# Two networks in one program on one core: both ends of the expert layer rewritten, and gate and up weights loaded as 512 rows by 1024 columns

## The chip, the cores and the metric

The kernel runs on one core of a Trainium2 chip, in one launch. The metric is the device time of that launch in microseconds. Times "before" are the median of three runs; a profile is one execution of its own.

## What is computed

A first block (two layers of dilated attention and gated scans) feeds a second one. Each of the second block's two layers has a mixer (gated delta rule and sparse attention), then a feed-forward part: dense in layer 0, eight experts in layer 1. There are 256 tokens of 1024 features, all in float32. What the change touches is the end of layer 1:

```python
x = x + g_m * y
h = rms_norm(x, norm_ffn[l]) * (1.0 + sc_f) + sh_f
...
def moe_ffn(h, w_router, w1, w3, w2):
    logits = (h @ w_router).astype(jnp.float32)
    top_val, top_idx = lax.top_k(logits, TOP_K)            # TOP_K = 2 of N_EXPERTS = 8
    top_w = jax.nn.softmax(top_val, -1)
    combine = jnp.sum(jax.nn.one_hot(top_idx, N_EXPERTS, dtype=jnp.float32) * top_w[..., None], -2)
    out = jnp.zeros_like(h)
    for e in range(N_EXPERTS):
        out = out + combine[..., e:e + 1].astype(h.dtype) * swiglu(h, w1[e], w3[e], w2[e])
    return out
...
x = x + g_f * f
```

`swiglu(h, w1, w3, w2)` is `(silu(h @ w1) * (h @ w3)) @ w2`, with a hidden width of 3584. The weights of one expert are 44 MB.

## The kernel before

**Weights.** All weights pass through RING, seven slots of 2 MB in SBUF. SP issues one DMA per slot, in the order in which TensorE uses them, and waits on `item_used` until the block that held the slot seven blocks ago is used up (L2847). A gate or up block is 1024 rows by 512 columns of a matrix whose rows are 3584 floats long, so each piece that lies together in memory is 2 KB. A down block is 512 whole rows of 1024 floats, 4 KB each.

**Routing.** At the end of the mixer DVE gates the product with GATE_ROW and adds it to X, one tile of 128 tokens at a time (L2282, L2284). Then `pe_entry`, `act_entry` and `dve_entry` make h: ACT squares X and sums, ACT and DVE form one over the root of the mean, DVE makes a diagonal matrix of it (DIAG), TensorE multiplies X by the diagonal and transposes by it (L1320), and ACT and DVE apply scale and shift while they take the result out of PSUM into HT. TensorE multiplies HT by `router_w` (L2292). DVE finds the two best experts of each token (L2312 to L2330), and TensorE counts tokens and finds each one's place in its expert's list (L2297 to L2301). DVE sorts the experts by their number of tokens (`rank_key`, `rank_sorted`, `rank_i`). With `ranked` SP reads the first and the last expert of that order into registers (L2834) and issues the first expert blocks. DVE forms the places by rank, the selection matrices SEL (L2411) and all weights, and clears ACC (L2392); all engines meet in `phase(..., "ffn")`; TensorE gathers the tokens by a matmul with SEL (L2435), and ACT takes them out into HTG (L2442).

**A turn.** One turn handles a pair of experts, one with many tokens and one with few: 64 tokens each side by side ("wide", L2555 and L2584), and up to 64 more (turn 0) or 32 more (later turns) of the first one ("extra", L2568 and L2594). Here there are four turns: turn 0 is written out, the others are one loop. A turn goes over seven slices of 512 hidden columns. For each: gate (bank 0 of PSB), up (bank 1), with the extra part of both in bank 2; ACT applies silu (L2643), DVE multiplies (L2682), TensorE transposes (L2575), ACT copies (L2651), and down of the slice before adds into PSA. Six blocks a slice, 42 a turn, 168 in all. Bank 3 is for odd jobs ("misc"): the last turn's rows are scattered back into ACC through it (L2450, added by DVE at L2456), SELW is transposed and the next turn's tokens are gathered. In the last turn a gather is made for a turn that doesn't come.

**The end.** After the loop all engines meet again, four scatters run, DVE adds them to ACC, multiplies ACC by GATE_ROW (L2701), adds it to X (L2703), and SP stores X, 1 MB, in one DMA (L2870).

## Time and profile before

| what | us |
|---|---|
| median of three runs | 2612.45 (2610.32 to 2614.62) |
| the profiled execution, its own time | 2612.26 |
| its span, first to last instruction | 2610.5 |
| TensorE busy | 2460.1 (94%) |
| VectorE (DVE) busy | 614.0 (24%) |
| ScalarE (ACT) busy | 455.7 (17%) |

The span is what the views below divide; the execution's own time is 1.8 us longer. "Busy" counts instructions of an engine, not its sequencer's waits. In the rows DMA share is the mean busy share of the 16 DMA engines, and PEclk the granted share of TensorE's full clock. A float32 matmul stands as two rows of the trace.

### The profile page before, as it was taken

Reading aid. Unit: us, or ns where it says so; the run is one execution under the profiler, and the core shown is the slowest. Engines: PE = TensorE matmul, PEld = TensorE weight load, DVE = VectorE, ACT = ScalarE, POOL = GpSimd, SP = SyncE. Lnnn points to the kernel's source line nnn. Section 1 sums busy time; section 2 is a strip of 40 time slices with the busy share of each in tenths; the row PEclk is TensorE's granted clock in tenths of the full one; section 3 lists DMA queues with packets and bytes.
Section 4 is the critical chain, followed back from the end, with each engine's and each line's share of the span. In section 5 each row is a group of like instructions: output and inputs, shape, how many; then the busy total and the mean of one; then the engine's idle time right before and its main releaser. Section 6 shows DMA issues by size and latency. Waiting matters only on the chain.

```text
span 2610.5 us, 36347 instructions
## 1 busy us (share of the span) xinstructions
PE 2460.1 (94%) x15945; PEld 1437.8 (55%) x15945; DVE 614.0 (24%) x1457; ACT 455.7 (17%) x949; POOL 48.2 (2%) x67
## 2 busy tenths in 40 slices
PE   7999999999999999999999999799999889989987
PEld 5754776756685547777677655444443334333333
DVE  1241556713444320000144332300000001001001
ACT  1321123322213310000122142200010000001000
POOL 3300000000000000000000000000000000000000
PEclk9999899998999999999999999799999999999999
DMA  8633633327224137434532521399999999999995
GB/s 255 127 129 105 233 133 137 129 105 258 67 99 161 65 111 276 151 140 175 190 89 98 194 93 37 112 393 394 394 393 394 393 394 394 391 396 388 389 393 212
DMA packets 258237, 586.58 MB, mean 225 GB/s; under 512 B 14592, under 2 KB 16720, under 8 KB 258080
## 3 DMA queue, kind: packets, MB, share of 16 engines
q1 hardware_dynamic: 254304, 576.93, 60.2%
q0 software_dynamic: 3376, 5.94, 1.4%
q8 instruction: 130, 2.13, 0.3%
q10 hardware_dynamic: 400, 1.36, 0.2%
q14 instruction: 27, 0.22, 0.0%
HBM read 583.14 MB, written 1.06 MB: 224 GB/s over the span
## 4 chain that ended last, share of the span: by engine, by line
PE 84%; DMA 8%; SPq 3%; DVE 2%; ACT 1%; issue 1%; DVEq 1%; ACTq 0%
PE PSA L325 15%; PE PSB L2555 12%; PE PSA L340 10%; PE PSB L2489 7%; DMA RING<-in_w_moe 7%; PE PSA L2584 5%; PE PSA L2471 4%; PE PSB L2568 4%; PE PSA L699 3%; SPq L2847 3%; PE PSA L1278 2%; PE PSA L1901 2%; PE PSA L2594 2%; PE PSB L1470 1%; PE PSA L1852 1%
## 5 line engine op out<-in xcount | busy, mean ns | idle before, releaser
L2555 PE MATMUL PSB<-RING,Y 128*64 128x512 f32 x1792 | 399.9, 599 | 41.1 <-issue 20.8
L325 PE MATMUL PSA<-RING,HT 128*128 128x512 f32 (+1 forms) x896 | 392.5, 587 | 8.6 <-ACT Y L1441 5.0
L340 PE MATMUL PSA<-HT,RING 128*128 128x256 f32 x1216 | 277.8, 389 | 8.6 <-DMA RING<-in_w_in_ab 4.2
L2555 PEld LDWEIGHTS PSB<-RING,Y 128*64 128x64 f32 x1792 | 133.2, 138 | 270.4 <-issue 258.0
L325 PEld LDWEIGHTS PSA<-RING,HT 128*128 128x128 f32 x896 | 165.7, 191 | 183.2 <-issue 178.0
L340 PEld LDWEIGHTS PSA<-HT,RING 128*128 128x128 f32 x1216 | 235.0, 195 | 45.1 <-issue 11.7
L2584 PE MATMUL PSA<-RING,ROW 128*64 128x512 f32 x896 | 198.4, 595 | 5.6 <-issue 4.3
L2489 PE MATMUL PSB<-HT,RING 128*128 128x256 f32 x896 | 199.8, 381 | 2.0 <-DMA RING<-in_w_dense 2.0
L2489 PEld LDWEIGHTS PSB<-HT,RING 128*128 128x128 f32 x896 | 171.2, 191 | 37.2 <-issue 12.4
L2682 DVE TENSOR_TENSOR ROW<-ROW,PSB 128x512 f32<-128x512 f32 (+2 forms) x56 | 28.2, 504 | 589.7 <-PE PSB L2555 553.0
L2568 PE MATMUL PSB<-RING,Y 128*32 128x128 f32 (+1 forms) x3136 | 132.9, 289 | 0.0
L2568 PEld LDWEIGHTS PSB<-RING,Y 128*32 128x32 f32 (+1 forms) x3136 | 103.8, 114 | 52.3 <-issue 39.0
L2584 PEld LDWEIGHTS PSA<-RING,ROW 128*64 128x64 f32 x896 | 64.5, 137 | 120.2 <-issue 118.4
L2651 ACT ACTIVATE ROW<-PSB 128x512 f32<-128x512 f32 (+2 forms) x56 | 25.1, 450 | 503.0 <-PE PSB L2575 502.9
L2471 PE MATMUL PSA<-RING,PROJ 128*128 128x512 f32 x224 | 100.5, 592 | 0.0
L2508 DVE TENSOR_TENSOR PROJ<-PROJ,PSB 128x256 f32<-128x256 f32 x28 | 11.8, 421 | 277.2 <-PE PSB L2489 277.2
L2643 ACT ACTIVATE ROW<-PSB 128x512 f32<-128x512 f32 (+2 forms) x56 | 25.2, 450 | 283.9 <-PE PSB L2555 213.3
L1278 PE MATMUL PSA<-RING,small 128*32 128x512 f32 x384 | 57.1, 748 | 11.8 <-DVE X L709 5.0
L699 PE MATMUL PSA<-RING,HT 128*128 128x512 f32 x128 | 61.3, 634 | 5.1 <-ACT HT L383 5.1
L2471 PEld LDWEIGHTS PSA<-RING,PROJ 128*128 128x128 f32 x224 | 42.6, 190 | 42.1 <-issue 40.7
L2594 PE MATMUL PSA<-RING,ROW 128*32 128x512 f32 (+1 forms) x448 | 65.6, 597 | 0.0
L353 ACT ACTIVATE PROJ<-PSA 128x1024 f32<-128x1024 f32 x33 | 33.7, 1021 | 158.7 <-PE PSA L340 80.6
(444 smaller groups left out, 2256.8 us busy)
## 6 DMA issues: line engine op xcount, KB each, us to landing
RING<-in_w_moe SPq DMA_DIRECT2D x168, 2048.0 KB, 20.1
RING<-in_w_ada SPq DMA_DIRECT2D x24, 2048.0 KB, 8.1
RING<-in_w_dense SPq DMA_DIRECT2D x21, 2048.0 KB, 11.9
RING<-in_w_in SPq DMA_DIRECT2D x20, 2048.0 KB, 11.6
RING<-in_w_in_c SPq DMA_DIRECT2D x15, 2048.0 KB, 8.0
RING<-in_w_in_ab SPq DMA_DIRECT2D x10, 2048.0 KB, 15.6
RING<-in_w_out SPq DMA_DIRECT2D x4, 2048.0 KB, 7.8
RING<-in_w_out_ab SPq DMA_DIRECT2D x3, 2048.0 KB, 7.8
```

The source lines that it names most:

```text
L325: mm = pe.matmul(PSA[:, lane[k], 512 * t:512 * t + cols], HT[:, c, P * t:P * t + P], W[:, c, 0:cols], start=(c == 0), stop=(c == KC - 1))
L340: mm = pe.matmul(PSA[:, lane[k], S * j:S * j + S], W[:, c, P * j:P * j + P], HT[:, c, :], start=(c == 0), stop=(c == KC - 1))
L699: mm = pe.matmul(PSA[:, t, 512 * hf:512 * hf + 512], YT4[:, c, P * t:P * t + P], W[:, c, 512 * hf:512 * hf + 512], start=(first and c == 0 ...
L1278: mm = pe.matmul(PSA[r:r + 32, lane[k], 512 * a:512 * a + 512], cT[:, c:c + 1].broadcast_to([P, 32]), W[:, c, :], start=(c < 4), stop=(c > ...
L1901: mm = pe.matmul(PSA[:, t, 512 * hf:512 * hf + 512], YMT[:, 4 * n + c, P * t:P * t + P], W[:, c, 512 * hf:512 * hf + 512], start=(n == 0 a ...
L2471: mm = pe.matmul(PSA[:, t, 512 * hf:512 * hf + 512], HID[k % 2][:, P * t:P * t + P], W[:, q, 512 * hf:512 * hf + 512], start=(k == 0), sto ...
L2489: mm = pe.matmul(PSB[:, 2 * which + k % 2, 0:S], W[:, c, P * q:P * q + P], HT[:, c, :], start=(c == 0), stop=(c == KC - 1))
L2555: mm = pe.matmul((UP if up else GATE)[WIDE * which:WIDE * which + WIDE, :], HTG[:, c, WIDE * which:WIDE * which + WIDE], W[which][:, c, :] ...
L2568: mm = pe.matmul(BOTH[ec * j:ec * j + ec, c0:c0 + pw], HTG[:, c, P:P + ec], W[:, c, pw * j:pw * j + pw], start=(c == 0), stop=(c == KC - 1))
L2584: mm = pe.matmul(OUT[0][WIDE * which:WIDE * which + WIDE, 512 * hf:512 * hf + 512], HIDT[0][:, g % 2, q, WIDE * which:WIDE * which + WIDE] ...
L2594: mm = pe.matmul(OUT[1][ec * j:ec * j + ec, 512 * hf:512 * hf + 512], hid[:, b, j, :], W[0][:, q, 512 * hf:512 * hf + 512], start=(g == 0 ...
L2847: sp.dma_start(slot_view(j), src).then_inc(sem(f"slot_loaded{j % SLOTS}"), 16)
```

## The change

**Blocks and stages.** The seven slices are grouped in stages (0,1), (2,3), (4,5), (6). In a stage of two slices a gate or up block is 512 rows by 1024 columns, for both slices at once, so that its pieces are 4 KB; two such blocks per expert and matrix follow each other (`kh` = 0, 1). The last slice keeps the old shape. Gate and up of a stage use banks 0 and 1 of PSB, one for each slice, one after the other; bank 2 holds the extra part of both slices. Silu and product of the extra part are one instruction for both slices.

**Start.** The sums for scale and shift move ahead of the mixer's last product (`dve_moe_prepare`), where `router_w` is multiplied by the scale. Logits are taken from X itself, transposed but not normalized; DVE scales them per token by `rms_x` and adds `router_shift`. The second tile's gating and adding are done in halves. Counts are computed first and waited for alone, and `rank_key` follows. Weights of the tokens come behind the first selection. Clearing ACC and the meetings of all engines are gone; ACC is a copy of X instead.

**Rows.** DVE multiplies each turn's result by GATE_ROW as it takes it out of PSUM, where ACT and DVE copied it before.

**End.** The last turn is written out on its own. It gathers nothing. Its last two down blocks are loaded in two halves of 512 columns each, and gating, scattering, adding and storing go by halves and quarters.

```diff
+        STAGES = [range(g, min(g + 2, GROUPS)) for g in range(0, GROUPS, 2)]
         turn_items = []
-        for g in range(GROUPS):
-            turn_items += [(1, "gate", g), (0, "gate", g), (1, "up", g), (0, "up", g)]
-            turn_items += [(1, "down", g - 1), (0, "down", g - 1)] if g else []
-        turn_items += [(1, "down", GROUPS - 1), (0, "down", GROUPS - 1)]
+        for u, stage in enumerate(STAGES):
+            for kind in ("gate", "up"):
+                turn_items += [(which, kind, (u, kh)) for kh in range(len(stage)) for which in (1, 0)]
+            if u:
+                turn_items += [(which, "down", g) for g in STAGES[u - 1] for which in (1, 0)]
+        turn_items += [(which, "down", g) for g in STAGES[-1] for which in (1, 0)]
...
+        def dve_moe_prepare(dve):
...
+            dve.tensor_tensor(ROUTED, router_w[:, :, :], md[:, 0:8].unsqueeze(2).broadcast_to([P, KC, N_EXP]), ALU.mult)
+            dve.drain()
+            dve.tensor_reduce(router_shift, ROUTED.rearrange("p c e -> p e c"), AX.X, ALU.add)
+            dve.tensor_tensor(router_w[:, :, :], router_w[:, :, :], md[:, 8:16].unsqueeze(2).broadcast_to([P, KC, N_EXP]), ALU.mult)
...
         def pe_router(pe):
+            need(pe, "gate_spread")
             for t in range(NT):
+                for hf in range(2):
+                    if t == 0 and hf == 0 or t == 1:
+                        need(pe, "x_ready")
+                    for c in range(4):
+                        mm = pe.transpose(PSB[:, 2 * t + hf, P * c:P * c + P], X[:, t, 512 * hf + P * c:512 * hf + P * c + P], ident)
+                    mm.then_inc(sem("h_turned"), 1)
...
             need(pe, "chosen")
+            for t in range(NT):
+                mm = pe.matmul(COUNTS, CF[:, C_ONE:C_ONE + P], chosen[:, t, :], start=(t == 0), stop=(t == NT - 1))
+            mm.then_inc(sem("places"), 1)
...
+                dve.scalar_tensor_tensor(logits[:, t, :], PSA[:, 0, 512 * t:512 * t + N_EXP], rms_x[:, t:t + 1], router_shift,
+                                         ALU.mult, ALU.add)
...
-            def first_wide(kind, g):
...
+            def first(kind, u, kh):
...
+                if kind == "gate" and kh == 0:
+                    if u:
+                        pe.wait_ge(sem("moe_turned_taken0"), each(turn, STAGES[u - 1][-1]))
+                        pe.wait_ge(sem("moe_turned_taken1"), staged(turn, u - 1))
...
+                if kind == "up" and kh == 0:
+                    pe.wait_ge(sem("moe_silu0"), each(turn, STAGES[u][-1]))
+                per = KC // n
+                for i in range(n):
+                    for c in range(per * kh, per * kh + per):
+                        for which in range(2):
+                            mm = pe.matmul(WIDE_BANKS[i][WIDE * which:WIDE * which + WIDE, :],
+                                           HTG[:, c, WIDE * which:WIDE * which + WIDE], W[which][:, c - per * kh, 512 * i:512 * i + 512],
+                                           start=(c == 0), stop=(c == KC - 1))
                 mm.then_inc(sem("item_used"), 1)
...
+            for u, stage in enumerate(STAGES):
+                for kind in ("gate", "up"):
+                    for kh in range(len(stage)):
+                        first(kind, u, kh)
...
+                turned_wide(u)
+                for n, g in enumerate(STAGES[u - 1] if u else ()):
+                    if u == len(STAGES) - 1 and not end:
+                        misc(SCATTERS + 1 + n)
+                    down(g)
+                turned_extra(u)
+            if not end:
+                misc(SCATTERS + 3)
+                down(GROUPS - 1)
+                return
+            for hf in range(2):
+                pe.wait_ge(sem(f"last_columns{hf}"), 32)
+                down_wide(GROUPS - 1, (512 * hf,), False)
+                down_extra(GROUPS - 1, (512 * hf,)).then_inc(sem("last_rows"), 1)
+            pe.wait_ge(sem("misc_free"), pieces(turn, SCATTERS + 1))
+            for piece in LAST_PIECES:
+                pe.wait_ge(sem("moe_rows"), turn + (piece % 2 + 1))
+                scatter_piece(pe, piece, piece).then_inc(sem("last_rows"), 1)
...
-                        src = w[:, :, 512 * g:512 * g + 512].rearrange("a (k p) n -> p (a k) n", p=P)
+                        u, kh = g
+                        rows_, cols = D // len(STAGES[u]), 512 * len(STAGES[u])
+                        src = w[:, rows_ * kh:rows_ * kh + rows_, 1024 * u:1024 * u + cols].rearrange("a (k p) n -> p (a k) n", p=P)
...
+            for n, piece in enumerate(LAST_PIECES):
+                t, cols = piece // 2, slice(512 * (piece % 2), 512 * (piece % 2) + 512)
+                sp.wait_ge(sem("result"), n + 1)
+                sp.dma_start(out[0].rearrange("(t p) f -> p t f", p=P)[:, t, cols], ACC[:, t, cols]).then_inc(sem("out_stored"), 16)
```

**Order on TensorE, routing, before.** CF,X and G_BACK,X are transposing matmuls of X, router_w,HT the logits, small,CF the places and last the counts, HT,X the gathers.

```order
L1901 MATMUL PSA<-RING 128x512 x24
L1312 MATMUL PSA<-CF,MODB 128x128 x8
L1320 MATMUL PSB<-G_BACK,X 128x128 x16
L2292 MATMUL PSB<-router_w,HT 128x8 x16
L2297 MATMUL PSB<-small,CF 128x8
L2298 MATMUL PSB<-small,CF 128x8
L2299 MATMUL PSB<-small,CF 128x8
L2301 MATMUL PSB<-small,CF 128x8 x2
L2435 MATMUL PSB<-HT,X 128x192 x16
```

The same place in the change:

```order
L1905 MATMUL PSA<-RING 128x512 x24
L2320 MATMUL PSB<-CF,X 128x128 x8
L2323 MATMUL PSA<-small,CF 128x8
L2330 MATMUL PSA<-router_w,HT 128x8 x8
L2320 MATMUL PSB<-CF,X 128x128 x8
L2330 MATMUL PSA<-router_w,HT 128x8 x8
L2335 MATMUL PSA<-small,CF 128x8 x2
L2337 MATMUL PSA<-small,CF 128x8
L2338 MATMUL PSA<-small,CF 128x8
L2339 MATMUL PSA<-small,CF 128x8
L2341 MATMUL PSB<-CF,MODB 128x128 x8
L2493 MATMUL PSB<-HT,X 128x192 x16
```

The first tile is transposed and multiplied on its own, the counts (x2) stand ahead of the places, and the gate row's eight matmuls moved from ahead of the transposes to behind the places.

**Order on TensorE, one slice of turn 0, before** (gate wide and extra, up wide and extra, transposes, down wide and extra, transposes of the extra part):

```order
L2555 MATMUL PSB<-RING,Y 64x512 x16
L2568 MATMUL PSB<-RING,Y 64x256 x16
L2555 MATMUL PSB<-RING,Y 64x512 x16
L2568 MATMUL PSB<-RING,Y 64x256 x16
L2575 MATMUL PSB<-CF,ROW 128x128 x4
L2584 MATMUL PSA<-RING,ROW 64x512 x16
L2594 MATMUL PSA<-RING,ROW 64x512 x8
L2575 MATMUL PSB<-CF,ROW 128x128 x2
```

In the change, from the second half of gate to the end of a stage of two slices:

```order
L2628 MATMUL PSB<-RING,Y 64x512 x16
L2637 MATMUL PSB<-RING,Y 64x256 x16
L2628 MATMUL PSB<-RING,Y 64x512 x16
L2637 MATMUL PSB<-RING,Y 64x256 x16
L2628 MATMUL PSB<-RING,Y 64x512 x16
L2637 MATMUL PSB<-RING,Y 64x256 x16
L2646 MATMUL PSB<-CF,PROJ 128x128 x8
L2662 MATMUL PSA<-RING,ROW 64x512 x16
L2676 MATMUL PSA<-RING,PROJ 64x512 x8
L2662 MATMUL PSA<-RING,ROW 64x512 x16
L2676 MATMUL PSA<-RING,PROJ 64x512 x8
L2653 MATMUL PSB<-CF,PROJ 128x128 x4
```

Passes and transposes keep their number and shape for two slices; two rounds of transposes became one of twice the length, and both down passes stand together.

## Rows read from the trace of the kernel before

**Rows 1.** Part 2 of the page, GB/s in 40 slices of the span.

```profile
GB/s 255 127 129 105 233 133 137 129 105 258 67 99 161 65 111 276 151 140 175 190 89 98 194 93 37 112 393 394 394 393 394 393 394 394 391 396 388 389 393 212
```

**Rows 2.** Windows of 100 us: busy (instructions) by engine, PEclk, DMA share, GB/s.

```profile
1800.00:1900.00 100.00, 100.00 (x568) 41.58 (x569) 3.33 (x6) 8.09 (x17) 0.00 (x0) 1.00 1.04 395
2200.00:2300.00 100.00, 92.21 (x802) 38.83 (x802) 4.30 (x8) 6.43 (x14) 0.00 (x0) 1.00 1.04 392
```

**Rows 3.** Windows of 5 us, columns as in rows 2.

```profile
2030.00:2035.00 5.00, 4.26 (x29) 1.24 (x27) 0.00 (x0) 0.28 (x1) 0.00 (x0) 1.00 1.05 387
2045.00:2050.00 5.00, 4.88 (x24) 1.74 (x26) 0.00 (x0) 0.00 (x0) 0.00 (x0) 1.00 1.03 411
```

**Rows 4.** DMA issues, part 6 of the page: KB each, us to landing.

```profile
RING<-in_w_moe SPq DMA_DIRECT2D x168, 2048.0 KB, 20.1
```

**Rows 5.** Timeline, routing: start, length, engine, line, instruction, [idle before <-releaser].

```profile
1643.64 1.23 DVE L2282 TENSOR_TENSOR Y<-PSA,MODB 128x1024 f32<-128x1024 f32 x1 [17.83 <-PE PSA L1901]
...
1650.62 1.22 DVE L2282 TENSOR_TENSOR Y<-PSA,MODB 128x1024 f32<-128x1024 f32 x1 [4.45 <-PE PSA L1901]
...
1654.41 1.28 ACT L673 ACT_TABLE_LOAD   x1
...
1662.47 5.49 PE L2292 MATMUL PSB<-router_w,HT 128*128 128x8 f32 x32 [1.11 <-ACT HT L1344]
1668.00 0.17 DVE L2312 COPY small<-PSB 128x16 f32<-128x16 f32 x1 [6.50 <-PE PSB L2292]
...
1671.97 1.00 PE L2301 MATMUL PSB<-small,CF 128*128 128x8 f32 x4
...
1673.51 0.17 DVE L2349 SCALAR_TENSOR_TENSOR small<-PSB,CF 128x8 f32<-128x8 f32 x1 [0.41 <-issue]
...
1676.29 85.18 SPq L2847 DMA_DIRECT2D RING<-in_w_moe  x18
```

**Rows 6.** Windows at the end of the stream, columns as in rows 2.

```profile
2574.00:2579.00 5.00, 5.00 (x28) 1.43 (x28) 0.00 (x0) 0.00 (x0) 0.00 (x0) 1.00 0.56 229
2579.00:2581.00 2.00, 2.00 (x19) 1.06 (x12) 0.00 (x0) 0.28 (x1) 0.00 (x0) 1.00 0.17 70
```

**Rows 7.** Timeline of TensorE, turn 0.

```profile
1683.51 7.68 PE L2435 MATMUL PSB<-HT,X 128*128 128x192 f32 x32 [10.54 <-DVEq L286]
1692.28 7.09 PE L2555 MATMUL PSB<-RING,Y 128*64 128x512 f32 x32 [1.09 <-ACT Y L2442]
...
1778.49 7.09 PE L2555 MATMUL PSB<-RING,Y 128*64 128x512 f32 x32
...
1810.69 7.09 PE L2555 MATMUL PSB<-RING,Y 128*64 128x512 f32 x32
...
1924.04 7.09 PE L2555 MATMUL PSB<-RING,Y 128*64 128x512 f32 x32 [0.95 <-ACT Y L2442]
```

**Rows 8.** Timeline of TensorE, a slice of turn 2.

```profile
2167.37 7.09 PE L2555 MATMUL PSB<-RING,Y 128*64 128x512 f32 x32
2174.39 1.98 PE L2450 MATMUL PSB<-MODB,HT 128*128 128x512 f32 x4
2176.30 1.95 PE L2568 MATMUL PSB<-RING,Y 128*32 128x128 f32 x64
...
2196.81 3.65 PE L2555 MATMUL PSB<-RING,Y 128*64 128x512 f32 x16
```

**Rows 9.** TensorE's waits from 1690 us on: us in total, times, longest.

```profile
PE PSB L2555 <- issue: 20.8, 10, 3.7
```

**Rows 10.** Timeline from 2555 us to the end.

```profile
2556.41 0.60 ACT L2643 ACTIVATE ROW<-PSB 128x512 f32<-128x512 f32 x1 [8.38 <-PE PSB L2555]
...
2567.20 0.69 DVE L2682 TENSOR_TENSOR ROW<-ROW,PSB 128x512 f32<-128x512 f32 x1 [29.61 <-PE PSB L2555]
...
2593.17 7.13 PE L2450 MATMUL PSB<-MODB,HT 128*128 128x512 f32 x16 [0.98 <-ACTq L286]
...
2606.02 0.39 SPq L2870 DMA_DIRECT2D result<-X  x1
```

More of the change, by code:

```diff
@@ new lines, in dve_router, with by_rank @@
+            dve.drain()
+            halves = [slice(0, 4), slice(7, 3, -1)]
+            def by_rank(to, src):
+                for t in range(NT):
+                    dve.tensor_tensor(PERMUTED[:, t, :, :], PERMUTE, src[:, t, :].unsqueeze(1).broadcast_to([P, N_EXP, N_EXP]), ALU.mult)
+                dve.drain()
+                for which in range(2):
+                    dve.tensor_reduce(to[which][:, :, 0:4], PERMUTED[:, :, halves[which], :], AX.X, ALU.add)
+                dve.drain()
+            by_rank(t_place, e_place)
@@ L2332, in dve_router @@
+            dve_select(dve, 0)
+            dve.drain().then_inc(sem("select"), 1)
+            need(dve, "act_output")
             dve.tensor_scalar(top_w[:, :, 0], top_w[:, :, 1], 1.0, None, ALU.add)
@@ L2699, in dve_moe_end @@
-        def dve_moe_end(dve):
-            for t in range(NT):
-                dve.tensor_tensor(ACC[:, t, :], ACC[:, t, :], GATE_ROW, ALU.mult)
-            dve.drain()
-            dve.tensor_tensor(X[:, :, :], X[:, :, :], ACC, ALU.add)
+            if not end:
+                dve.wait_ge(sem("item_used"), used(turn, (0, "down", GROUPS - 1)))
+                for k in range(2):
+                    e = dve.tensor_tensor(YG[k], OUT[k], GATE_ROW, ALU.mult)
+                e.then_inc(sem("moe_rows"), 1)
+                return
```

503 lines of the change are left out of this document (273 added, 230 removed).

## The prediction

> **What bounds the kernel now.** I read the slices of the page first, then the same span in windows, the waits, the order of time on TensorE, and last the two ends of the expert layer. From slice 27 on the DMA engines are full and the rate stands near 393 GB/s, while before that it jumps between 37 and 276 [rows 1]: the last third of the kernel is one stream of expert weights. In windows of 100 us the stream shows a DMA share of 1.04 and 392 to 395 GB/s, and TensorE is 92 to 100% busy beside it [rows 2]. So two limits lie close together, and which of them is the longer has to be worked out. In windows of 5 us the stream has two rates: 387 GB/s where gate and up blocks move (rows of 2 KB) and 411 GB/s where down blocks move (rows of 4 KB) [rows 3]. A block is 2048 KB [rows 4], 2.097 MB, so it takes 5.42 us at the one rate and 5.11 us at the other. I use 5.12 for the second, since a neighbouring window of down blocks shows 410.
>
> The stream now: 112 blocks of gate and up by 5.42 and 56 of down by 5.12 make 893.8 us. It begins 1.9 us behind the first issue at 1676.29 [rows 5], at 1678.2. It thins out at 2574 and ends near 2579.9 [rows 6]: between 2574 and 2579 the share is 0.56, so about half of the DMA engines finish some 5 us behind the others. That is 901.7 us in all, 7.9 more than the blocks alone; I keep these 7.9 as they are.
>
> TensorE: in turn 0 a slice of 512 hidden columns takes from 1778.49 to 1810.69, 32.20 us [rows 7], where its six blocks need 4 x 5.42 + 2 x 5.12 = 31.9 us. Turn 0 is bound by TensorE by a hair, and seven slots hide it. In a later turn a slice goes from 2167.37 to 2196.81, 29.4 us, of which one scatter is 1.98 [rows 8]: 27.5 without it. The gathers of a later turn are as many matmuls as the first ones, of 160 columns and not 192: at most 7.68 x 160 / 192 = 6.4 us [rows 7]. A later turn is then 7 x 27.5 + 4 scatters of 1.9 + 0.6 + 6.4 = 207.1 us at most, against 223.4 us of blocks. So turns 1 to 3 are bound by the DMA, by 16 us or more each. The waits say the same: ahead of gate and up TensorE stood idle for 20.8 us named "issue", ten times, up to 3.7 us each [rows 9]. I read them as blocks whose last part had not landed.
>
> **The change, part by part.** *Blocks.* Per turn 24 of the 28 gate and up blocks get rows of 4 KB; the seventh slice, alone in its stage, keeps 4 blocks with rows of 2 KB. No row shows a block of 4 KB rows that lie 14 KB apart in memory, as these will; down's rows lie end to end. Bounds: the down block's 5.12 us, and 5.42 us as now. I take 5.12: the two kinds of block differ in the length of their rows first of all, and a step of 5.7% for twice the length looks like a fixed cost per row; whether stride has a part in it no row tells. A turn is then 4 x 5.42 + 38 x 5.12 = 216.2 us. The last two down blocks come as four halves with rows of 2 KB, 2.71 us each, 0.6 more together. Stream: 4 x 216.2 + 0.6 = 865.4 us, 28.4 less.
>
> The Trainium skill ("DMA: Bandwidth & Descriptors", Specifications) gives 512 B as the smallest transfer at line rate, by which rows of 2 KB and of 4 KB would cost the same and this part would bring nothing, the time of rival A. This case's trace disagrees, with 387 against 411 GB/s.
>
> *Start of the layer.* Both kernels stand alike until DVE takes the second row tile at 1650.62. Now [rows 5]: gate and add 2.5 us, square, and root with its table load of 1.28 us at 1654.41; then the diagonal, transposing matmuls and evictions until 1662.47, 5.49 us of logits, the choice on DVE from 1668.00 until TensorE counts at 1670.6, 2.4 us of places and counts up to 1672.97, and from the rank key at 1673.51 2.8 us to the first load, at 1676.29. New: gate and add in halves, 3.05 us, to 1653.7. Square to 1654.9. One eviction on ACT once TensorE has turned the tile, to 1656.4, and root with its table load (1.6) to 1658.0; logits of the first tile run before, from X itself, and those of the second end near 1659.2. On DVE the first tile's seven small operations, 0.25 to 0.3 us each with their drain, take 2.0 to 1660.0, and the second's six 1.8, to 1661.8. Counts alone (the x4 row, 1.0 us) are waited for, not the places: 1.4 less than the 5.7 us from 1670.60 to 1676.29. First load at **1666.1, 10.2 us earlier**. Bounds: 1664 if the second tile's logits and the root hide one another better, 1669 if the second tile's logits take all of the present 5.49 us.
>
> TensorE's start: before, the gathers begin at 1683.51 [rows 7], when DVE has cleared ACC and all engines have met. New: select is ready near 1667.4, TensorE is past the gate row's matmuls (3.44) at 1668.0, gathers 7.7, last eviction about 1.1: 1676.9. The first pair of blocks lands at 1666.1 + 1.9 + 2 x 5.12 + 0.6 = 1678.9 and is what the first matmul waits for, 13.4 us earlier than 1692.28. The preparation moved ahead of the mixer's last product is about 2 us of DVE beside an idle time of 17.8 us [rows 5]: nothing. If that cover were gone it would cost its 2 us.
>
> *Two slices at once.* Matmuls and transposes are the same in number and shape. Gate and up now share two banks, so TensorE waits for ACT's two silu (0.60 each [rows 10]) ahead of up, beside the extra pass of 1.95 us [rows 8]: hidden. DVE's two products (0.69 each) stand beside the same pass: hidden with 0.4 to spare. Only the copy of the extra slices is bare, ahead of the next gate, three times a turn: about 0.7 us, 2 a turn. The wait at a turn's end for the last gather (0.95 [rows 7]) goes, since a down pass now stands behind it. A later turn is about 208 us of TensorE against 216.2 of blocks, so still 8 us loose. In turn 0 TensorE needs 32.2 us a slice and the blocks only 30.7; over the turn the stream gains 11 us and runs into the seven slots. At turn 0's end, near 1913, some 47.5 blocks would have landed where 42 are used, of 49 allowed, and TensorE frees slots in steps of 7.0 and 3.6 us. I charge **4 us** of empty queue; bounds 0 and 9.
>
> *End.* Last landing: 1666.1 + 1.9 + 865.4 + 7.9 + 4 = 2545.3. The four halves are the last 10.8 us of it, so the down pair before them lands at 2534.5. From there TensorE is the path: 7.0 + 1.9 for that pair, 0.3 transposes, two half passes of 4.45, four scatters 7.1 [rows 10], one add 0.8, and a last store of a quarter of the present 1 MB. That one takes 4.5 us from 2606.02 to the span's end; less 0.79 MB at 387 GB/s it is 2.5, with the wait 2.8. That makes 28.8. **Span 2563.3.** Now 30.6 us lie between the last landing and the end, in the new order 18.0: the gathers for a turn that doesn't come and DVE's gating and adding of whole rows are gone from there.
>
> The profiled execution is 2612.26 us beside a span of 2610.5, 1.8 more, and 0.2 under the median of 2612.45. Forecast: 2563.3 + 1.8 + 0.2 = **2565.3 us**, 47 less: 28.4 from rows, 10.2 from the start, 12.6 from the end, minus 4 held back.
>
> **Rivals.** A, *strided 4 KB rows cost what strided 2 KB rows cost.* For it: every block at 387 GB/s is strided, every one at 411 is not. Against: the rates split by size just as well. All 96 blocks at 5.42: 28.8 more, the 4 us of empty queue gone: 2590. B, *half of the gain*: 96 x 0.15 = 14.4 more, 2 less held: 2578. The Trainium skill ("DMA: Bandwidth & Descriptors", Why small descriptors are slow) has a fixed cost of some 3 cycles beside one per 32 B for each packet; for 64 and 128 such beats that makes a 4 KB row 2.2% cheaper per byte, an estimate of 5.30 us a block and of a time near 2581. The rows show 5.7%.
>
> C, *slower than before: TensorE becomes the bound because the handoffs at the shared banks are bare.* TensorE's own work is 230.8 (turn 0, from 1692.28 to 1924.04 less the wait [rows 7]) + 3 x 207.1 - 6.4 (the last turn has no gathers) = 845.7; from 1678.9 that ends at 2524.6, plus 7.1 and 3.6: 2535. Were every silu, product and copy of a stage bare, a double stage would lose 1.2 + 1.4 + 1.2 + 1.9 + 0.6 for semaphores = 6.3 us, a single one 3.5: 12 x 6.3 + 4 x 3.5 = 90, span 2625, time 2627. It decides against the forecast only from 2 us a stage on, and loses to the present kernel from 4.7. Against it: the extra pass is there in the new order too, and it is longer than what it hides.
>
> D, *the ends bring less*: the first load no earlier than 1672 and the store serial. About 8 us more, 2573.
>
> **Numbers.** Forecast 70%, A 9%, B 12%, C 3%, D 6%. The range of 2554 to 2586 holds the forecast's own bounds (start, empty queue, tail: 9 down, 10 up), B and D, and leaves out A and C and some edges. About 0.2%, 5.2 us, is what a measurement of this kernel can tell from no change. Faster 0.94, same 0.03, slower 0.03: only C, or A together with a failed start, comes near 2607.
>
> **What would show it.** The first load near 1666; gate and up windows at 410 GB/s outside the seventh slice, or at 387 (A); 24 of 28 gate and up blocks 128x4x1024; TensorE's waits on ACT about 0.7 us at each stage end, and more than 2 would be C; DMA share below 1 late in turn 0; four scatters as the last TensorE work, and some 8 us from the last down matmul to the last store's issue. A time above 2595 makes the main step wrong.

## The result and the profile after

Median 2569.09 us (2565.43 to 2573.34, four runs) against 2611.39 (2604.19 to 2614.62, four runs) for the kernel before beside it: ratio 0.9842 (0.9821 to 0.9864), 42 us less. The forecast was 2565.3 us. The profiled execution took 2573.34 us, its span 2571.5. Medians and ratios here and below leave out one execution of narrow (5091.50 us) and one of down_small_unrolled (5830.81 us), which took about twice as long as the others of the same kernel.

I read the page first. Its rate by slices of the span (part 2), and the count of packets:

```profile
GB/s 257 131 123 115 237 135 140 119 117 231 100 70 161 66 98 285 140 166 128 140 205 83 68 226 69 1 390 409 401 405 386 409 401 408 408 401 409 409 398 277
DMA packets 210444, 586.56 MB, mean 228 GB/s; under 512 B 14672, under 2 KB 16800, under 8 KB 210288
```

Where the kernel before streamed at 393 [rows 1], this one streams at 401 to 409 in most slices, with 48 thousand packets fewer (258237 before). One slice, the thirty-first, has 386. Windows tell why (busy and instructions by engine, PEclk, DMA share, GB/s):

```profile
2020.00:2025.00 5.00, 5.00 (x24) 1.99 (x25) 0.00 (x0) 0.00 (x0) 0.00 (x0) 1.00 1.02 409
2025.00:2030.00 5.00, 5.00 (x80) 2.69 (x78) 0.00 (x0) 0.00 (x0) 0.00 (x0) 1.00 1.03 411
1850.00:1900.00 50.00, 49.22 (x272) 22.78 (x270) 1.11 (x2) 4.64 (x10) 0.00 (x0) 1.00 1.03 404
1900.00:1950.00 50.00, 50.00 (x389) 20.31 (x386) 3.73 (x4) 2.71 (x6) 0.00 (x0) 1.00 1.01 393
1930.00:1940.00 10.00, 10.00 (x98) 4.23 (x94) 0.08 (x1) 1.47 (x3) 0.00 (x0) 1.00 0.99 388
1950.00:2000.00 50.00, 49.11 (x501) 22.22 (x499) 5.77 (x13) 3.43 (x7) 0.00 (x0) 1.00 1.00 390
```

Inside a turn gate and up blocks now move at 409 to 411 GB/s, down's rate [rows 3]. From about 1900 to 2000 us the share falls from 1.03 to 0.99 or 1.00 while TensorE is 98 to 100% busy: the queue waits for slots. That is what the forecast charged 4 us for. It lies later than the forecast had it: turn 0 ends at 1918.5, and most of the stretch is in turn 1.

The start of the layer, in order of time (start, length, engine, line, instruction, idle before and releaser); it answers to [rows 5, 7]:

```profile
1658.76 0.69 DVE L2289 TENSOR_TENSOR Y<-PSA,MODB 128x512 f32<-128x512 f32 x1 [4.45 <-PE PSA L1905]
...
1660.89 0.69 DVE L2291 TENSOR_TENSOR X<-X,Y 128x512 f32<-128x512 f32 x1
...
1662.93 0.60 ACT L2354 ACTIVATE HT<-PSB 128x512 f32<-128x512 f32 x1
...
1663.54 1.28 ACT L676 ACT_TABLE_LOAD   x1
...
1663.58 2.67 PE L2330 MATMUL PSA<-router_w,HT 128*128 128x8 f32 x16 [0.97 <-ACT HT L2354]
...
1665.16 0.17 DVE L2373 COPY small<-PSA 128x8 f32<-128x8 f32 x1 [1.29 <-ACT small L678]
...
1668.91 1.02 PE L2335 MATMUL PSA<-small,CF 128*128 128x8 f32 x4 [2.66 <-DVEq L2388]
...
1669.97 0.17 DVE L2392 SCALAR_TENSOR_TENSOR small<-PSA,CF 128x8 f32<-128x8 f32 x1 [0.86 <-PE PSA L2335]
...
1672.83 0.40 SPq L2957 DMA_DIRECT2D RING<-in_w_moe  x1
...
1674.62 5.48 PE L2493 MATMUL PSB<-HT,X 128*128 128x192 f32 x32
1685.79 8.41 PE L2628 MATMUL PSB<-RING,Y 128*64 128x512 f32 x32 [5.70 <-DMA RING<-in_w_moe]
```

The first load stands 14.1 us behind the second tile's gating, where it stood 25.7 behind it. The second tile's logits (2.67 us for 16 instructions) run beside the table load of 1.28 us. DVE begins its choice when the root is done (L678), with the first tile, and so does not wait for them. The first expert matmul then waits for its blocks alone, 13.0 us behind the first load.

The second tile itself is late, though: 1658.76 against 1650.62. The program is the same up to there but for some sums that moved into an idle time. The page's row of a line of the mixers' part shows what differs, first in the kernel before, then in this one:

```profile
L1278 PE MATMUL PSA<-RING,small 128*32 128x512 f32 x384 | 57.1, 748 | 11.8 <-DVE X L709 5.0
```

```profile
L1282 PE MATMUL PSA<-RING,small 128*32 128x512 f32 x384 | 64.0, 827 | 11.8 <-DVE X L712 5.0
```

The same 384 matmuls take 827 ns and not 748 each, with the same idle time ahead of them. Between 1275 and 1300 us the granted clock was 0.86 before and is 0.66 here, a mixture of TensorE's two levels of 1.2 and 2.4 GHz. Whether the change causes that is a question for a second run.

The end of the layer, answering to [rows 10]:

```profile
2552.09 3.65 PE L2662 MATMUL PSA<-RING,ROW 128*64 128x512 f32 x16
2555.67 1.06 PE L2676 MATMUL PSA<-RING,PROJ 128*32 128x512 f32 x8
2556.67 3.65 PE L2662 MATMUL PSA<-RING,ROW 128*64 128x512 f32 x16
...
2560.25 1.06 PE L2676 MATMUL PSA<-RING,PROJ 128*32 128x512 f32 x8
2561.25 7.13 PE L2508 MATMUL PSB<-MODB,HT 128*128 128x512 f32 x16
...
2563.98 5.48 SPq L2992 DMA_DIRECT2D result<-PROJ  x4
...
2568.42 0.69 DVE L2514 TENSOR_TENSOR PROJ<-PROJ,PSB 128x512 f32<-128x512 f32 x1 [1.03 <-PE PSB L2508]
```

Four stores follow the scatters' pieces, the last 2.4 us from the span's end. Windows at the end of the stream, answering to [rows 6]:

```profile
2549.00:2551.00 2.00, 2.00 (x18) 0.56 (x18) 0.00 (x0) 0.00 (x0) 0.00 (x0) 1.00 0.50 194
2551.00:2553.00 2.00, 2.00 (x18) 0.48 (x8) 0.00 (x0) 0.28 (x1) 0.00 (x0) 1.00 0.17 67
2553.00:2554.00 1.00, 1.00 (x8) 0.43 (x6) 0.00 (x0) 0.00 (x0) 0.00 (x0) 1.00 0.00 0
```

So the last data land near 2553.0, 18.5 us from the end. From the first data (1.9 us behind the first load, 1674.7) the stream took 878.3 us. TensorE's waits from 1676 us on, in all, how often, longest:

```profile
PE PSB L2628 <- DMA RING<-in_w_moe: 19.5, 12, 5.7
PE PSB L2628 <- ACT PROJ L2754: 6.8, 9, 0.9
PE PSA L2662 <- issue: 5.4, 7, 1.3
PE PSB L2628 <- issue: 4.8, 1, 4.8
```

The bare copy at a stage's end (`ACT PROJ L2754`) is waited for nine times, 0.76 us each on average. The 20.8 us named "issue" in ten waits [rows 9] have become one of 4.8 us, and it stands in a place of its own, at the jump from turn 1 back to the loop's head:

```profile
2123.95 1.92 PE L2676 MATMUL PSA<-RING,PROJ 128*32 128x512 f32 x16
2130.63 9.56 PE L2628 MATMUL PSB<-RING,Y 128*64 128x512 f32 x32 [4.76 <-issue]
```

The pass behind it takes 9.56 us and not 7.09. The kernel before, whose loop jumps back twice, has two such places:

```profile
2144.70 5.78 PE L2555 MATMUL PSB<-RING,Y 128*64 128x512 f32 x18 [3.74 <-issue]
...
2370.30 8.78 PE L2555 MATMUL PSB<-RING,Y 128*64 128x512 f32 x32 [3.60 <-issue]
```

These are the two longest of the ten waits in [rows 9], all of which I had read as blocks that had not landed. No run here settles what the other eight, 13.5 us together, waited for.

### The profile page after: what moved, and what is told of

It is laid out like the page before. It is cut to its first block, busy times and chain, and to the rows that moved or that the text cites. A ratio compares the mean times of both kernels' runs of the same rounds, so it can differ in the third digit from the quotient of the medians.

```text
span 2571.5 us, 36173 instructions
## 1 busy us (share of the span) xinstructions
PE 2453.3 (95%) x15899; PEld 1436.9 (56%) x15899; DVE 607.9 (24%) x1440; ACT 441.0 (17%) x912; POOL 48.3 (2%) x67
## 4 chain that ended last, share of the span: by engine, by line
PE 86%; DMA 8%; ACT 2%; DVE 1%; SPq 1%; issue 1%; DVEq 0%; ACTq 0%
PE PSA L328 15%; PE PSB L2628 13%; PE PSA L343 11%; PE PSB L2547 8%; DMA RING<-in_w_moe 7%; PE PSA L2662 5%; PE PSB L2637 4%; PE PSA L2529 4%; PE PSA L702 3%; PE PSA L1282 2%; PE PSA L1905 2%; PE PSA L2676 2%; PE PSB L2508 1%; PE PSB L1474 1%; PE PSA L1856 1%; PE PSB L1880 1%
## 5 line engine op out<-in xcount | busy, mean ns | idle before, releaser
L2784 DVE TENSOR_TENSOR PROJ<-PROJ,PSB 128x512 f32<-128x512 f32 x28 | 18.2, 684 | 556.4 <-PE PSB L2628 556.4
L1282 PE MATMUL PSA<-RING,small 128*32 128x512 f32 x384 | 64.0, 827 | 11.8 <-DVE X L712 5.0
L2676 PE MATMUL PSA<-RING,PROJ 128*32 128x512 f32 (+1 forms) x448 | 65.8, 597 | 0.0
L2748 ACT ACTIVATE ROW<-PSB 128x512 f32<-128x512 f32 x28 | 15.4, 595 | 281.6 <-PE PSB L2646 281.6
L2738 ACT ACTIVATE PROJ<-PSB 128x512 f32<-128x512 f32 x28 | 15.4, 595 | 279.5 <-PE PSB L2628 279.5
```

Source lines behind the costliest of these rows:

```text
L1282: mm = pe.matmul(PSA[r:r + 32, lane[k], 512 * a:512 * a + 512], cT[:, c:c + 1].broadcast_to([P, 32]), W[:, c, :], start=(c < 4), stop=(c > ...
L2676: mm = pe.matmul(OUT[1][ec * j:ec * j + ec, col:col + 512], hid[:, b, j, :], W[:, q, col:col + 512], start=(g == 0 and b == 0), stop=(g == ...
```

## The experiments

All kernels below are the changed one with one edit. "Layer" is the time of the profiled execution from the second tile's gating by GATE_ROW to the end of the span: it leaves out the part whose clock wanders. The ratio is against the kernel before, run beside each.

| kernel | second tile at | layer | median | ratio (95%) |
|---|---|---|---|---|
| before | 1650.62 | 959.9 | 2611.39 | 1 |
| after | 1658.76 | 912.7 | 2569.09 | 0.9842 (0.9821 to 0.9864) |
| after_again | 1651.04 | 913.5 | 2566.54 | 0.9828 (0.9809 to 0.9847) |
| after_third | 1659.55 | 912.2 | 2567.48 | 0.9821 (0.9800 to 0.9842) |
| narrow | 1650.80 | 936.8 | 2589.36 | 0.9913 (0.9882 to 0.9943) |
| ends_only | 1654.1 | 936.8 | 2594.72 | 0.9939 (0.9921 to 0.9958) |
| whole_end | 1644.40 | 914.3 | 2565.07 | 0.9824 (0.9793 to 0.9855) |
| less_turn0 | 1658.50 | 908.7 | 2565.04 | 0.9799 (0.9769 to 0.9828) |
| unrolled | 1655.36 | 911.9 | 2562.16 | 0.9796 (0.9774 to 0.9817) |
| more_pe | 1649.97 | 914.3 | 2566.27 | 0.9797 (0.9761 to 0.9832) |
| down_long | 1653.35 | 1024.5 | 2677.76 | 1.0255 (1.0237 to 1.0273) |
| down_small | 1648.42 | 928.2 | 2579.46 | 0.9881 (0.9858 to 0.9904) |
| down_small_unrolled | 1648.25 | 916.0 | 2564.51 | 0.9819 (0.9797 to 0.9841) |
| half_long | 1651.81 | 979.8 | 2633.62 | 1.0079 (1.0060 to 1.0097) |

**The changed kernel again (after_again, after_third).** No edit.

> The changed kernel once more, for its spread. From DVE's gating of the second row tile (the last point that both kernels share) to the end it took 912.7 us, the kernel before 959.9. The 8.1 us by which the changed profile came later to that point lie in code that is the same in both. Theory: they come and go with the granted clock of the short adaptive matmuls, so the stretch up to that point is 1651 to 1659 us in any run, and the stretch behind it is 913 within 3. Rival: the change slows the early part (merged semaphores), then that point is at 1657 or later every time.

> The changed kernel once more, beside the two versions of this call: 2566 to 2569 us, ratio about 0.983, and 912 to 914 us from the second tile's gating to the end.

The layer is 912.2 to 913.5 us in three profiles, while the second tile comes anywhere between 1644.40 and 1659.55 over all kernels that share the part ahead of it. after_again puts the second tile at 1651.04 with the same code, so the 8 us by which the first profile was late there are no work of the change. They go with the granted clock. Its mean up to 1600 us is 0.973 in whole_end, whose second tile is the earliest, 0.968 in the kernel before and in after_again (1650.62 and 1651.04), and 0.963 to 0.964 in after, after_third and less_turn0, the three latest; over all fourteen profiles the two are correlated at -0.98. The row of the 384 matmuls follows only loosely (691 ns with the tile at 1648.25 in down_small_unrolled, 724 with 1644.40 in whole_end, 827 with 1658.76 in after, 790 with 1659.55 in after_third): one group of instructions does not stand for the whole part. That the spread of the changed kernel's own medians (2566.5 to 2569.1) has the same source is likely, but only one execution of each was profiled.

**Rows of 2 KB in the new order (narrow).**

```diff
-                    sp.dma_start(slot_view(j), src).then_inc(sem(f"slot_loaded{j % SLOTS}"), 16)
+                    for h in range(2):
+                        part = slice(512 * h, 512 * h + 512)
+                        sp.dma_start(slot_view(j)[:, :, part], src[:, :, part]).then_inc(sem(f"slot_loaded{j % SLOTS}"), 16)
```

> Only the load of the gate and up blocks changes: each block of 512 rows by 1024 columns comes as two DMAs of 512 columns, rows of 2 KB instead of 4 KB. Everything else is the changed kernel. Theory S (the stream of weights is the path, and a block's price follows from the length of its rows): 96 blocks go from 5.12 back to 5.42 us, 28.8 more, less about 4 of empty queue in turn 0: the expert layer at 937 to 940, the time 23 to 28 above the changed kernel. Rival (two slices at once, or the ends, bring the gain): no change.

A window inside a turn, columns as above:

```profile
2030.00:2035.00 5.00, 3.03 (x72) 1.94 (x70) 0.00 (x0) 1.47 (x3) 0.00 (x0) 1.00 1.05 387
```

The rate of gate and up is 387 GB/s again, and the layer is 24.1 us longer, 24.0 against the mean of the three profiles of the changed kernel. The blocks, their order, the stages and all of TensorE's work are the same. Two things differ: the row length, and that a block now comes as two DMAs. The next run has the short rows with one DMA a block and takes the same time, so it is the row length. By the forecast's prices it is 96 x 0.30 = 28.8 us less the 4 held back, 24.8.

**The ends alone (ends_only).** One slice per stage, blocks of 1024 rows by 512 columns, all else new.

```diff
-        STAGES = [range(g, min(g + 2, GROUPS)) for g in range(0, GROUPS, 2)]
+        STAGES = [range(g, g + 1) for g in range(GROUPS)]
```

> The new ends with blocks of 1024 rows by 512 columns and one slice at a time, as before; the rest is the changed kernel. Theory S: the stream is that of narrow, so the time is within 3 us of narrow's, 18 to 24 us under the kernel before (start 11.6, end 12). Rival (joining two slices saves or costs TensorE time that counts): it differs from narrow by more than 5 us.

Also 936.8 us, 23.1 less than the kernel before. Rows and ends thus account for 24.1 + 23.1 = 47.2 us, and the pairing of slices, apart from the rows that it allows, for nothing: narrow and ends_only differ in it alone, and in the number of DMAs per block. That the two differences each cost something and cancel is not excluded, but nothing points to it. The medians of the two are 5.4 us apart (2589.36 and 2594.72), which by time alone would have spoken for the rival. In the profiles the second tile is 3.3 us later in ends_only and the rest of the difference (936.8 and 936.8) is nil, so I go by the layer.

**The last blocks whole (whole_end).**

```diff
-            load_items(last, range(PER_TURN - 2))
+            load_items(last, range(PER_TURN))
```

> The last two down blocks are loaded whole and multiplied in one go, the rest is the changed kernel. The down pass of 8.9 us then stands behind the last landing as one, and DVE's gating (two of 0.65 and two of 0.65) is bare ahead of the scatters. Theory: 3 us more, from the last TensorE pass to the end 13 us instead of 11. Rival: the halves bring nothing, since TensorE is behind the loads there: 0.

The layer is 1.5 us longer than the changed kernel's mean of 912.8, where 3 were expected, near the measurement's own spread of 1.3. Its end:

```profile
2537.98 7.09 PE L2662 MATMUL PSA<-RING,ROW 128*64 128x512 f32 x32 [0.90 <-issue]
2545.00 1.92 PE L2676 MATMUL PSA<-RING,PROJ 128*32 128x512 f32 x16
2548.43 7.10 PE L2508 MATMUL PSB<-MODB,HT 128*128 128x512 f32 x16 [1.50 <-DVE MODB L2817]
```

Whole, the last down pass has waited 0.9 us (named "issue"; its block ends near 2537.5), and the scatters wait 1.5 us for DVE's gating of whole rows; in halves both are covered. From the last data to the end it is some 21 us here and 18.5 in the changed kernel, 2.5 less for the halves. But their rows of 2 KB are loaded more slowly: the stream is some 1 us shorter here. The halves save the difference of the two. So most of the new end's gain must lie elsewhere, in the gathers left out and the four stores; no run separates these.

**A lighter turn 0 (less_turn0).** It leaves out the odd chunks of the extra pass of gate and up in turn 0, half of those products.

```diff
-                    for c in range(per * kh, per * kh + per):
+                    for c in range(per * kh, per * kh + per, 1 if begun else 2):
```

> In turn 0 the extra pass of gate and up multiplies every second chunk of features only, which leaves out half of these products for the extra tokens. TensorE's turn 0 gets some 25 us shorter and is no longer behind the stream. Theory S with held blocks: the queue never runs dry in turn 0, 3 to 5 us less, no more. Theory T (TensorE's work is the path): 20 us or more less.

```profile
1900.00:1950.00 50.00, 49.92 (x442) 21.07 (x438) 6.86 (x12) 2.16 (x5) 0.00 (x0) 1.00 1.03 409
```

Turn 1 starts 11 us earlier (248.8 us behind the second tile, 259.8 in the changed kernel), the queue no longer runs dry, and 4.1 us of that reach the end (908.7 against 912.8). The windows give the same: 409 and not 393 GB/s from 1900 to 1950 us, 408 and not 390 from 1950 to 2000, which is 4.2 us of stream. This is the held-back time, measured to about the spread of 1.3 us.

**The loop written out (unrolled).**

```diff
-                    last = turn_count(pe)
-                    with pe.Fori(1, last) as turn:
-                        pe_moe_turn(pe, turn)
-                    pe_moe_turn(pe, last, True)
+                    for turn in (1, 2):
+                        pe_moe_turn(pe, turn)
+                    pe_moe_turn(pe, 3, True)
```

> Turns 1 and 2 are written out instead of looped (a case with more than four turns is left out), so no engine jumps back. In the changed profile TensorE stands 4.8 us at the jump between turns 1 and 2 and then runs 10 matmuls slowly, though the block has landed 4 us before. Theory: this idle time belongs to the jump and is gone, and the time stays within 2 us, since the slots hide it. Rival: the idle time stays (a late block). Rival T: 5 to 7 us less.

```profile
2121.01 1.92 PE L2676 MATMUL PSA<-RING,PROJ 128*32 128x512 f32 x16
2122.86 7.09 PE L2628 MATMUL PSB<-RING,Y 128*64 128x512 f32 x32
```

The pause is gone, turn 2 starts 4.4 us earlier (467.5 behind the second tile against 471.9), and by turn 3 the two kernels are level (686.4 and 686.5): blocks that had not landed take its place. The layer gains 0.9 us. Turn 1 alone, from 259.7 to 467.5, is 207.8 us of TensorE with 3.2 us of waits in it (2.0 for ACT's copies, 1.2 named "issue"); the forecast had 208.

**More work on TensorE (more_pe).** Wide transposes three times over in turns 1 to 3.

```diff
-                    for q in range(4):
+                    for q in range(4) if not begun else (0, 1, 2, 3) * 3:
```

> In turns 1 to 3 each transpose of the wide part is done three times over, 8.2 us more of TensorE in each turn, 25 in all. Theory S: a later turn had about 208 us of TensorE against 216 of blocks, so nearly all of it goes into the slack: 0 to 6 us more. Theory T: 25 us more.

24 transposes take 2.84 us, the 8 of the changed kernel 1.09. Turn 2 starts 477.3 us behind the second tile and not 471.9, turn 3 at 691.5 and not 686.5, and the layer ends 1.5 us later. That is 1.75 us more for each pair of slices and 6.1 a turn: 18.4 us in all (L2646 is busy for 34.1 us and not 15.7), and not the 25 that I expected. TensorE's idle time ahead of gate, up and down falls from 32.0 to 17.0 us at the same time. So 18 us of work beside a stream that ends the kernel cost 1.5, which is near the spread: turns 1 to 3 had that slack.

**Pieces of 16 KB for down (down_long).** If 4 KB beat 2 KB, longer pieces may beat 4 KB. Partition p takes rows 4p to 4p+3 of a down block, one run of 16 KB in memory. Hidden columns then have to be taken four apart.

```diff
-                        src = w[:, 512 * g:512 * g + 512, :].rearrange("a (k p) n -> p (a k) n", p=P)
+                        src = w[:, 512 * g:512 * g + 512, :].rearrange("a (p k) n -> p (a k) n", p=P)
...
-                        mm = pe.transpose(WIDE_BANKS[i][:, P * q:P * q + P], ACTED[0][:, i, P * q:P * q + P], ident)
+                        mm = pe.transpose(WIDE_BANKS[i][:, P * q:P * q + P], ACTED[0][:, i, :].rearrange("p (s q) -> p q s", q=4)[:, q, :], ident)
...
-                                           W[0][:, c - per * kh, 512 * i + pw * j:512 * i + pw * j + pw],
+                                           W[0][:, c - per * kh, 512 * i:512 * i + 512].rearrange("p (s q) -> p q s", q=4)[:, pw // P * j:pw // P * j + pw // P, :],
```

> Each partition takes four neighbouring rows of a down block, 16 KB in one piece, instead of four rows 128 apart; the hidden columns are transposed in the matching order, with a stride of four floats in the transposes and in the extra pass of gate and up. If a row costs a fixed time beside its bytes (2 KB 5.42, 4 KB 5.12 us a block, so some 0.3 at 4 KB), a down block falls to about 4.9: 56 x 0.22 = 12 us less stream, of which TensorE holds some back in turn 0: 6 to 10 us less. Rival: pieces are cut at 4 KB, no change. Rival: TensorE reads the strided columns slower, the extra pass grows from 1.95 or 3.6 us and turn 0 gets longer: same or slower.

```profile
2150.00:2155.00 5.00, 5.00 (x34) 1.93 (x34) 0.00 (x0) 0.55 (x1) 0.00 (x0) 1.00 1.02 436
```

```profile
1696.33 7.07 PE L2628 MATMUL PSB<-RING,Y 128*64 128x512 f32 x32
1703.22 7.43 PE L2637 MATMUL PSB<-RING,Y 128*64 128x256 f32 x32
```

Windows of 5 us with down blocks show 426 and 436 GB/s, so the rate goes on rising with the piece; the expectations below reckon with 436. But the extra pass, whose weights are the moving operand and are now read four elements apart, takes 7.43 us where it took 3.63. TensorE is the bound, and the layer 112 us longer. I had expected 6 to 10 us less; the second rival came true.

**The same with the order put right in the transposes (down_small, down_small_unrolled).** Gate and up read their weights as before; the extra transposes become small products with columns of the identity.

```diff
-                    for q in range(pw // P):
-                        mm = pe.transpose(EXTRA_BANK[:, i, P * q:P * q + P], ACTED[1][:, i, P * q:P * q + P], ident)
+                    some = ACTED[1][:, i, 0:pw].rearrange("p (s q) -> p q s", q=4)
+                    for j in range(parts):
+                        own = slice(ec * j, ec * j + ec)
+                        for q in range(4):
+                            mm = pe.matmul(EXTRA_BANK[own, i, ec * q:ec * q + ec], some[:, q, :], ident[:, own], start=True, stop=True)
```

> Down blocks in pieces of 16 KB per partition once more, but with the extra pass of gate and up left as it is: the order of the hidden rows is put right where it costs least, in the transposes. The wide ones read every fourth column, and the extra pass's one or two whole transposes per group of 512 become 8 (turn 0) or 16 (later turns) products of 64 or 32 columns with a part of the identity. Stream: a down block at 436 GB/s instead of 411 is 0.31 us less, 54 blocks: 16 us less if the transfer alone sets the turns. TensorE: by the run with tripled transposes, where 2.84 us stood for 24 of 128 columns (0.12 us each), a product of 32 columns costs between 0.03 us (a quarter) and 0.12 us (no cheaper), so 15 more for each of 7 groups is 3 to 12 us more per turn, of which 8 were absorbed when the turn was as long as the stream is now (220 us). Stream theory: 16 us less than the changed kernel beside it, if the products are 0.03 us. TensorE theory: between 6 us less and 12 us more, with TensorE and no longer the ring ending the waits. I expect 5 us less than the changed kernel, some 2563 us, and 907 us from the second tile to the end.

> The same with turns 1 to 3 written out instead of looped (what a fifth turn would need is left out), which takes TensorE's 4.8 us pause at the loop's end away. Under the changed kernel's stream this pause was hidden. Where TensorE bounds the turns it isn't: then 5 to 10 us less than the looped version beside it (two back edges). Where the stream bounds them: within 1 us of it. I expect 4 us less than the looped one.

```profile
2097.28 1.80 PE L2493 MATMUL PSB<-HT,X 128*128 128x160 f32 x12
...
2128.10 1.92 PE L2679 MATMUL PSA<-RING,PROJ 128*32 128x512 f32 x16
2134.69 1.96 PE L2628 MATMUL PSB<-RING,Y 128*64 128x512 f32 x3 [4.66 <-issue]
2140.22 9.54 PE L2628 MATMUL PSB<-RING,Y 128*64 128x512 f32 x29 [3.57 <-issue]
...
2185.18 2.53 PE L2656 MATMUL PSB<-CF,PROJ 128*32 128x32 f32 x64
```

I was wrong: down_small is 15 us longer than the changed kernel, not 5 shorter. The 32 small products of a pair of slices take 2.53 us, 0.08 each, between my bounds. TensorE becomes the bound of every turn: behind its first pass it waits for no block any more (in down_small_unrolled turns 1 and 2 are 214.0 and 214.1 us), turn 0 too, where the changed kernel had nothing left: turn 1 starts 8 us later. And a stream that runs 16 us shorter is of no use. The loop's jump now shows its price in full: 4.66 and 3.57 us of idle time, and 11.5 us for a pass of 7.09, at a granted clock of 0.50 between 2140 and 2145 us, the lower of its two levels. That is 12.6 us, and the two kernels' layers are 12.2 apart; I had expected 4, between 5 and 10 for two jumps, and there is one jump. Why it stands in two pieces no run shows. Written out, the kernel's time is level with the changed one (0.9819 and 0.9821, beside each other), and its layer 3.2 us longer (916.0 against 912.8).

**16 KB for the second expert's down blocks only (half_long).** Only the wide pass reads these, so the extra transposes stay. The wide ones become eight products with halves of the identity.

```diff
+                    some = ACTED[0][:, i, :].rearrange("p (s q) -> p q s" if which else "p (q s) -> p q s", q=4)
...
+                        mm = pe.matmul(WIDE_BANKS[i][:, P * q + WIDE * which:P * q + WIDE * which + WIDE], some[:, q, :], ident[:, own], start=True, stop=True)
```

> Between the two: only the down blocks of the second expert of each turn come in pieces of 16 KB per partition (these blocks are read by the wide pass alone, so the extra pass and its transposes stay as they are). The wide transposes become 8 products per group of 512 rows with halves of the identity, 64 columns each, in the place of 4 transposes of 128. Stream: 27 whole blocks, 0.31 us less each: 8 us less, as long as TensorE keeps up. TensorE: a turn of the unrolled kernel with small products took 214.1 us (its first matmuls at 2130.27 and at 2344.34) and was set by TensorE; without its small products (2.5 us for two groups, 0.4 before) the same turn would be 206 us. Four products more for each of 7 groups at 0.14 us (the transposes' 1.09 us for 8) are 4 us: 210 us, against 212.8 us for 42 blocks of 5.12 us less 7 of 0.31. So the stream should still set the turns. Stream theory: 905 us from the second tile to the end, 8 less than the changed kernel's 912 to 914, and some 2560 us. TensorE theory (the loop's pause of 12 us isn't made up for with so little left): 908 to 914.

```profile
1977.21 5.77 PE L2649 MATMUL PSB<-CF,PROJ 128*128 128x64 f32 x32
1982.77 0.64 PE L2656 MATMUL PSB<-CF,PROJ 128*128 128x128 f32 x2
1984.03 9.79 PE L2628 MATMUL PSB<-RING,Y 128*64 128x512 f32 x32 [0.62 <-ACT PROJ L2757]
...
2024.84 5.73 PE L2649 MATMUL PSB<-CF,PROJ 128*128 128x64 f32 x32
2030.50 8.75 PE L2665 MATMUL PSA<-RING,ROW 128*64 128x512 f32 x32
```

A miss by 75 us. A float32 product stands as two instructions and a transpose as one, and I had priced the product as a transpose: 16 products of 64 columns take 5.77 us, 0.36 each, against 0.14. Less the 1.09 us of transposes that they replace, 3.5 such pairs of slices add 16 us to a turn. The pass behind them takes 8.75 or 9.79 us and not 7.09, with a granted clock of 0.83 between 2030 and 2040 and of 0.72 between 1984 and 1994. So turn 1 takes 231.9 us (from 284.1 to 516.0 behind the second tile) where TensorE needed 207.8, and the faster stream waits for it. No run that does all of the work has a layer shorter than the changed kernel's by more than the spread of the measurement.

## Why the prediction was right

The layer, from the second tile's gating to the end, was forecast as 15.5 + 1.9 + 877.3 + 18.0 = 912.7 us. Measured: 14.1 + 1.9 + 878.3 + 18.5, with roundings 912.7. No term was off by more than 1.4 us. That the sums agree to a tenth is luck: the start came 1.4 us shorter, the stream 1.0 and the end 0.5 longer. The whole time alone would not have decided it either. Its median, 2569.1, lies between the forecast (2565.3) and rival D (2573) at equal distance, and the profiled execution is D's time. D falls by its own marks: the first load is 14.1 us behind the second tile's gating, where D had 21 or more, and four stores follow the pieces, the last 2.4 us from the end.

- **Rows of 4 KB**, 28.4 us less. Confirmed by the windows (409 to 411 GB/s) and by narrow, which gives 24.1 us back where 28.8 less the hold was forecast. Rival A (strided rows of 4 KB cost what strided rows of 2 KB cost) and B (half of it) fall with the same windows. The Trainium skill ("DMA: Bandwidth & Descriptors", Specifications) has the line rate reached from 512 B on; the runs disagree, with 387, 411 and 426 to 436 GB/s at 2, 4 and 16 KB. The fixed cost of some 3 cycles per packet of the same page of the Trainium skill (Why small descriptors are slow) would give, by my estimate, 2.2% from 2 to 4 KB; the windows show 5.7 to 6.2%, in both directions of the experiment.
- **The 4 us of empty queue.** less_turn0 gives back 4.1 us. This was the softest term, taken between 0 and 9, so its nearness is in part luck; and most of it lies in turn 1, not late in turn 0.
- **The start**, 10.2 us less: 11.6. Some 1.0 us of the difference lies ahead of the root: I gave ACT's one eviction there 1.5 us, and it took 0.60. The way from the counts to the first load took 3.9 us where I had 4.3. The second tile's logits are hidden behind the root and the first tile's choice, as forecast. The first matmul is 13.0 us behind the first load where 12.8 was forecast, and waits for its blocks, as said.
- **The end**, 12.6 us less: 12.1. That is how the sum came out; of its parts, the halves are worth 1.5 us by whole_end (2.5 at the end, less 1.0 in the stream), and I did not try the four stores and the missing gathers apart.
- **The pairing of slices** costs 0.76 us at a stage's end, nine times in the four turns (0.7, three times a turn, was forecast), and none of it reaches the end as far as narrow and ends_only tell. Rival C falls in the changed kernel: a turn of TensorE is 207.8 us where 208 was forecast. The rival was right as a mechanism, though: in down_long, down_small and half_long TensorE did become the bound, by other costs than bare handoffs.
- **The 7.9 us of the stream** that no block accounts for I kept whole and did not explain. They are still there, as less_turn0 shows: its stream takes 874.2 us, where the blocks and these 7.9 make 873.3. Part of them is the tail: the share is 0.50 and 0.17 in the last 4 us, and was 0.56 and 0.17 in the last 7 before [rows 6]. That the missing share is half of the DMA engines done early, as the prediction has it, is an inference from the mean; no row names the engines.

Where I was wrong without paying for it: the 20.8 us of "issue" waits [rows 9]. The longest two were the loop's jumps. They are covered by a stream that ends the kernel, and unrolled gained 0.9 us only. Had the turns been bound by TensorE, as in down_small, each might have cost 12 us, and my floor for TensorE's turns, made of busy time alone, would have been short by as much.

The measured median is 3.8 us above the forecast, and the profiled execution 8.0. In the profiled execution none of it is in the layer: it goes with the granted clock of the part ahead, which moved the second tile between 1644 and 1660 us in kernels with the same code there. For the median this is only likely.

## What to carry to other kernels

When a stream ends a kernel, look at its rate in short windows, one kind of block at a time: a difference of some per cent between kinds is a price list for a change of layout, and it held when the blocks were recut. Ask in the same breath how much time the engine beside it has left per turn, pauses of its sequencer included; here that was 7 us of 215, and every further gain for the stream that cost TensorE more than this was lost. Judge such a change from a mark inside the program (here the second tile) to the end: the whole program's time scatters by as much as the smaller terms of the sum.

## What the runs showed of the hardware

- The rate of 2 MB blocks rises with the piece: 387 GB/s with pieces of 2 KB, 409 to 411 with 4 KB, whether they lie end to end or 14 KB apart, and 426 and 436 in two windows with 16 KB.
- A float32 matmul whose moving operand is read four elements apart takes twice as long: 32 instructions of 256 columns 7.43 us, 3.63 when read in a row. The wide transposes take their stationary operand that way for 1.23 us per eight, 1.09 in a row.
- The jump back at the end of the loop over turns leaves TensorE idle for 3.6 to 4.8 us in the kernel before and in the changed one, and the pass behind it takes 8.8 to 9.6 us and not 7.1 (granted clock 0.50 from 2130 to 2135 us in the changed one). In down_small, where TensorE is the bound, the idle time is 4.7 and 3.6 us, and writing the loop out saves 12.2 us. Leaving the loop shows no such pause: in the changed kernel TensorE is idle there for 0.44 us, for a block.
- Behind runs of 16 float32 products with 64 columns (5.8 us of them) the granted clock was 0.72 and 0.83 in two windows of 10 us, though TensorE was busy before, but for 0.6 us ahead of the first, and in them. In down_small_unrolled, whose small products have 32 columns (64 in turn 0) and take 2.5 to 2.8 us at a time, no wide pass of 32 instructions takes longer than 7.1 us.
- The same 384 instructions of the mixers' part took between 691 and 827 ns each in fourteen profiles, and the mean granted clock up to 1600 us was between 0.963 and 0.973. The time up to the second tile went with that clock and moved by up to 15 us.
